# High and low weights of a merged product in alternating sets of two to four tile pairs

## The chip, the cores and the metric

One core of a Trainium2 chip runs the whole program once. The metric is the device time of that execution in microseconds (us), the median over several executions.

## The reference, cut to what matters

Two transformer blocks, one after the other, on 256 tokens of 1024 channels, all in float32. The first block has two layers (windowed attention, then a bidirectional retention), each with a gated feed-forward; the second has two layers of feed-forward, a three-branch mixer and another feed-forward:

```python
def swiglu_2(h, w_gate, w_up, w_down):
    return (jax.nn.silu(h @ w_gate) * (h @ w_up)) @ w_down
...
for l in range(DEPTH):
    x = x + 0.5 * swiglu_2(rmsnorm(x, ffn1_norm[l]), ffn1_w_gate[l], ffn1_w_up[l], ffn1_w_down[l])
    h = rmsnorm(x, mix_norm[l])
    proj = h @ w_in[l]
    ...
    x = x + 0.5 * swiglu_2(rmsnorm(x, ffn2_norm[l]), ffn2_w_gate[l], ffn2_w_up[l], ffn2_w_down[l])
```

Nearly all work is products of a 256-token activation with a large weight matrix. The hidden width of a feed-forward is 2816, so one feed-forward reads 1024x5632 and 2816x1024 weights.

## The kernel before

**Weights in two parts.** A float32 weight w is used as a high part `w_hi` (rounded by ScalarE, ACT) and a low part `w_lo` = w - w_hi (subtracted by VectorE, DVE). An activation has the same two parts. A product is high weight times high activation, plus high weight times low activation, plus low weight times high activation. Weights come in units: 4 chunks of 128 rows by 256 columns, one DMA of 512 KB into one of 4 slots (`raw`), from which ACT makes the slot's `w_hi` (line 1689) and DVE its `w_lo` (line 2328).

**A merged unit.** In the products `rg`, `rwo`, `gu1`, `dn1` of the first block and `gua`, `dna`, `memk`, `xr`, `yr`, `gub`, `dnb` of each layer of the second, the two activation parts lie so that one matmul takes both: it holds one 128x128 tile of `w_hi` and streams 512 columns, 256 of the high and 256 of the low activation (line 1086). These are called highs here. A low is a matmul that holds a tile of `w_lo` and streams the 256 high columns into the second half of the same bank (line 1097). A unit has 4 chunks k and 2 column blocks cb, so 8 tile pairs: 8 highs, a wait until DVE has made the unit's low weights (`unit_ready`, line 1009, semaphore lo_done), then 8 lows, the last of which counts the unit as used. Every matmul has its own weight load on the engine's load side (PEld).

**Which units there are.** `gua`, `gub`, `gu1` (gate and up of a feed-forward) have 11 iterations of 4 units; the first is written out, the other 10 are a loop on the chip. `dn1`, `dna`, `dnb` (down) have 2 iterations of 12 units, as a loop; the sixth and the twelfth unit of an iteration have 2 chunks, so 4 highs and 4 lows. `rg`, `rwo`, `xr`, `yr`, `memk` have 4 to 16 units. In `gua` and `gub` the sums of squares of the layer before (3 matmuls of line 1231) stand between units 2 and 3 of the first iteration. The first two units of `rg`, `gu1`, `gua`, `gub`, `xr` take chunk by chunk as the norm delivers them (`opens`), and the last unit of `rwo` goes by columns: 4 highs, 4 lows, 4 highs, 4 lows (lines 1042 and 1045).

**Order around it.** Each engine runs its own program in order. ACT and DVE split weights up to four units ahead of PE and take finished blocks of results in between; slots come free when PE has used a unit.

Of the kernel before, what the change touches and what calls it, by code (L numbers as in the profile page):

```python
# [26 lines left out]
P = 128  # L27
D = 1024
DC = D // P
S = 256  # L30
# [3 lines left out]
KCH = 4  # L34
# [336 lines left out]
def pooled_before(name, l):  # L371

    if name in SQUARED1:
        return 3 * (SQUARED1.index(name) - len(BOTH))
    return 3 * (len(SQUARED1) - len(BOTH) + SQUARED2.index(name) + l * len(SQUARED2))
# [7 lines left out]
def squared_before(name, l):  # L383

    first = [5 if n in BOTH else 4 for n in SQUARED1]
    if name in SQUARED1:
        return sum(first[:SQUARED1.index(name)])
    return sum(first) + 4 * SQUARED2.index(name) + l * 4 * len(SQUARED2)


def build(nc, a, out, const_at):
    J = JOBS
    st = ExitStack()
    with st:
        def sb(name, shape, dt=F32, on=st):
            return on.enter_context(nc.sbuf_tensor(name, shape, dt))

        def sem(name):
            return st.enter_context(nc.semaphore(name))
# [6 lines left out]
        w_hi = sb("w_hi", [P, SLOTS, KCH, COLS], F32R)  # L406
        w_lo = sb("w_lo", [P, SLOTS, KCH, COLS], F32R)
# [123 lines left out]
        units_used = sem("units_used")  # L531
# [143 lines left out]
        def norm_sums(n, half):  # L675

            return wk[:, 2 if half else 3, 0:S]
# [328 lines left out]
        def _(pe):  # L1006
            def unit_ready(job, l, it, p):

                pe.wait_ge(lo_done, job.split(l, it, p) + SLOTS + 1)
# [11 lines left out]
            def keep_busy(bank, n):  # L1021

                for _ in range(n):
                    pe.matmul(bank[:, 0:P], ident[:, :], ident[:, :], start=True, stop=True, skip_group_check=True)

            def product(name, l=None, hi=None, lo=None, tok=slice(0, S), rows_of=None, needs=None, normed=None, squared=False,
                        after=None, scaled=None, sums=None, merged=None, free=None,
                        sums_after=None, written=False, by_columns=False, busy=0):

                job = J[name]  # L1030
                per = job.body // job.per
                hi, lo = (h_hi, h_lo) if hi is None else (hi, lo)

                def one(it, start=0):
                    for p in range(start, job.body):
                        b, u = divmod(p, per)
                        if by_columns and (it, p) == (job.iters - 1, job.body - 1):
                            unit_ready(job, l, it, p)
                            for cb in range(2):
                                c = slice(cb * P, (cb + 1) * P)  # L1040
                                for k in range(job.unit_chunks[p]):
                                    pe.matmul(acc[:, b % 2, cb, :], w_hi[:, p % SLOTS, k, c], merged[:, :, u * KCH + k, tok], start=False, stop=False,
                                              skip_group_check=True)
                                for k in range(job.unit_chunks[p]):
                                    mm = pe.matmul(acc[:, b % 2, cb, S:2 * S], w_lo[:, p % SLOTS, k, c], merged[:, 0, u * KCH + k, tok], start=False,
                                                   stop=(k == job.unit_chunks[p] - 1), skip_group_check=True)
# [10 lines left out]
                        nk, s, last = job.unit_chunks[p], p % SLOTS, u == per - 1  # L1057
# [3 lines left out]
                        if tokens_major:  # L1061
                            unit_ready(job, l, it, p)
                            for n, r in enumerate(tokens_major):
                                packed = len(tokens_major) > 2
                                o = acc[:, b % 2, n // 2, (n % 2) * S:(n % 2) * S + S] if packed else acc[:, b % 2, n, 0:S]
                                for k in range(nk):
                                    x = slice(r * P, (r + 1) * P)
                                    kk = u * KCH + k
                                    for i, (xs, ws) in enumerate(((hi, w_hi), (hi, w_lo), (lo, w_hi))):

                                        mm = pe.matmul(o, xs[:, kk, x], ws[:, s, k, :],
                                                       start=(u == 0 and k == 0 and i == 0 and not (packed and n % 2)),
                                                       stop=(last and k == nk - 1 and i == 2), skip_group_check=packed)
                        else:
                            t = tok if not callable(tok) else tok(b)
                            outs = [acc[:, b % 2, cb, 0:t.stop - t.start] if merged is None else acc[:, b % 2, cb, :] for cb in range(2)]
                            opens = b == 0 and ((normed is not None and not isinstance(normed, tuple)) or (scaled is not None and isinstance(it, int)))
                            order = [(k, cb) for k in range(nk) for cb in range(2)] if opens else [(k, cb) for cb in range(2) for k in range(nk)]
                            for k, cb in order:
                                kk, c = u * KCH + k, slice(cb * P, (cb + 1) * P)  # L1080
                                if normed is not None and not isinstance(normed, tuple) and cb == 0 and b == 0:
                                    pe.wait_ge(h_ok, normed + kk + 1)
                                if scaled is not None and isinstance(it, int) and cb == 0 and b == 0 and kk % 2 == 0:
                                    pe.wait_ge(y_ok_c, scaled + kk // 2 + 1)
                                if merged is not None:
                                    pe.matmul(outs[cb], w_hi[:, s, k, c], merged[:, :, kk, t], start=(u == 0 and k == 0), stop=False,  # L1086
                                              skip_group_check=True)
                                else:
                                    for x in (hi, lo):
                                        pe.matmul(outs[cb], w_hi[:, s, k, c], x[:, kk, t], start=(u == 0 and k == 0 and x is hi), stop=False,  # L1090
                                                  skip_group_check=True)
                            unit_ready(job, l, it, p)
                            for cb in range(2):
                                o = outs[cb] if merged is None else outs[cb][:, S:2 * S]
                                x = hi if merged is None else merged[:, 0]
                                for k in range(nk):
                                    mm = pe.matmul(o, w_lo[:, s, k, cb * P:(cb + 1) * P], x[:, u * KCH + k, t], start=False,  # L1097
                                                   stop=(last and k == nk - 1), skip_group_check=True)
# [5 lines left out]
                if isinstance(normed, tuple):  # L1104

                    slot_free(job, l, 0, 0)
                    for half in range(2):
                        t = slice(half * S, half * S + S)
                        for p in range(per):
                            if not half:  # L1110
                                unit_ready(job, l, 0, p)
                            for cb in range(2):
                                for k in range(KCH):
# [5 lines left out]
                                    for i, (ws, xs) in enumerate(((w_hi, hi), (w_hi, lo), (w_lo, hi))):  # L1119
                                        mm = pe.matmul(acc[:, 0, cb, t], ws[:, p % SLOTS, k, c], xs[:, p * KCH + k, t],  # L1120
                                                       start=(p == 0 and k == 0 and i == 0),
                                                       stop=(p == per - 1 and k == KCH - 1 and i == 2), skip_group_check=True)
                            if half:
                                mm.then_inc(units_used, 1)
                    one(0, per)
                    for it in range(1, job.iters):
                        one(it)
# [95 lines left out]
            def pooled_sum(name, l=None):  # L1223

                pe.wait_ge(pooled, pooled_before(name, l) + 3)
                if name != "rwo":
                    pe.wait_ge(sqb_ok, squared_before(name, l) + 4)
                for n, src in enumerate((sq_of[:, 0, 0, :], sq_of[:, 1, 0, :], sq_of[:, 1, 1, :])):
                    if name == "rwo" and n:
                        pe.wait_ge(*((col_ok, 4) if n == 1 else (sqb_ok, squared_before(name, l) + 4)))  # L1230
                    mm = pe.matmul(norm_sums(None, 0), ones[:, :], src, start=(n == 0), stop=(n == 2))
                mm.then_inc(ss_ok, 1)
# [230 lines left out]
            def beside_queries(u):  # L1463
# [13 lines left out]
                if u == 6:  # L1477
                    query_sums(2)
                    partners(6)

            product("q0", tok=both, after=beside_queries, written=True)
            for k in range(3):
                side_modulation(k)
# [79 lines left out]
            for h in range(RH):  # L1563
# [3 lines left out]
                if h:  # L1567
# [3 lines left out]
                    after=lambda u: turn_y(RH - 1) if u == 0 else None)  # L1571
# [7 lines left out]
            for l in range(LAYERS2):  # L1579
# [10 lines left out]
                job = J["kvlru"]  # L1590
                slot_free(job, l, 0, 0)
                slot_free(job, l, 0, 1)
                for p in range(2):
                    unit_ready(job, l, 0, p)
                    for cb in range(2):
                        for k in range(KCH):
                            for i, (ws, xs) in enumerate(((w_hi, h_hi), (w_hi, h_lo), (w_lo, h_hi))):
                                mm = pe.matmul(acc[:, 1 - cb, 0, 0:S], ws[:, p, k, cb * P:(cb + 1) * P], xs[:, p * KCH + k, 0:S],
                                               start=(p == 0 and k == 0 and i == 0), stop=(p == 1 and k == KCH - 1 and i == 2))
                    mm.then_inc(units_used, 1)  # L1600
                for p in range(2, 4):
                    unit_ready(job, l, 0, p)
                    wh, wl = w_diag[:, p - 2, 0], w_diag[:, p - 2, 1]
                    for c in range(DC):
                        b = 2 * (p - 1) + c // 4
# [5 lines left out]
                        for i, (w, x) in enumerate(((wh, h_hi), (wh, h_lo), (wl, h_hi))):  # L1611
                            mm = pe.matmul(o, w[:, c * P:(c + 1) * P], x[:, c, mem], start=(i == 0), stop=(i == 2))
# [3 lines left out]
                for r in range(2):  # L1616
                    mm = pe.transpose(wk[:, 3, r * P:(r + 1) * P], v_T[:, r * P:(r + 1) * P], ident[:, :])
# [51 lines left out]
            job, l = J["dnb"], LAYERS2 - 1  # L1669
# [1557 lines left out]
```

## Time and profile before

| | |
|---|---|
| median of 3 runs | 2412.74 us (2411.22 to 2414.16) |
| profiled execution | 2409.69 us, of which the traced span is 2407.9 us |
| PE busy | 2370.9 us, 98% of the span, 14322 matmuls |
| DVE, ACT busy | 1557.6 us (65%), 1209.4 us (50%) |
| granted TensorE clock | 1.000 of full speed (2.4 GHz) as the mean over the span |

A profile's busy time of PE counts overlapping matmuls once. A matmul's own duration (start to end) is longer than its distance to the next one, because matmuls are pipelined.

### The profile page before, as it was taken

The numbers are of one execution on the slowest core, as the hardware profiler recorded it, in microseconds if no ns is written. First come the engines' busy times: TensorE is split into PE (matmuls) and PEld (weight loads), VectorE is DVE, ScalarE is ACT, GpSimd is POOL, SyncE is SP. The second block draws the span as 40 slices with busy tenths as digits, with TensorE's granted clock in tenths as the row PEclk, the third lists the DMA queues.
The fourth block names the chain that finished last, engine by engine and source line by source line (L and its number), as shares of the span: only waits on it lengthen the run. The fifth ranks groups of instructions, "written<-read, shape, count | busy, mean of one in ns | idle before, by whom it ended". The sixth has DMA issues, their size and how long they took to land.

```text
span 2407.9 us, 39768 instructions
## 1 busy us (share of the span) xinstructions
PE 2370.9 (98%) x14322; PEld 2029.7 (84%) x14322; DVE 1557.6 (65%) x2316; ACT 1209.4 (50%) x1783; POOL 158.1 (7%) x145
## 2 busy tenths in 40 slices
PE   8999999999999999999999999999999999999999
PEld 6756888888898868888888899998888889989887
DVE  5386665423474267766876858777677776777875
ACT  4365422222353234655554586565455556865553
POOL 3000100000000000000000013100000000221000
PEclk9999999999999999999999999999999999999999
DMA  9453755433363214656656655366566565545654
GB/s 332 135 184 128 228 154 162 143 107 96 99 193 96 88 53 154 204 163 195 201 173 193 192 168 176 130 181 193 178 191 193 180 196 167 183 130 158 200 174 149
DMA packets 388420, 398.39 MB, mean 165 GB/s; under 512 B 17344, under 2 KB 382432, under 8 KB 388304
## 3 DMA queue, kind: packets, MB, share of 16 engines
q1 hardware_dynamic: 381984, 377.67, 50.8%
q0 software_dynamic: 6320, 19.17, 2.6%
q8 instruction: 74, 1.21, 0.2%
q14 instruction: 42, 0.34, 0.1%
HBM read 395.73 MB, written 1.05 MB: 165 GB/s over the span
## 4 chain that ended last, share of the span: by engine, by line
PE 84%; DVE 5%; ACT 4%; issue 3%; POOL 2%; SPq 1%; DMA 1%; DVEq 0%; ACTq 0%; POOLq 0%
PE acc L1086 30%; PE acc L1097 23%; PE acc L1090 16%; PE acc L1163 2%; PE wk L1163 2%; ACT w_hi L1689 1%; DVE w_lo L2328 1%; SPq L795 1%; PE wk L1285 1%; PE acc L1639 1%; PE wk L1323 1%; PE acc L1323 1%; PE wk L1305 1%; POOL bias L994 1%; PE wk L1534 1%
## 5 line engine op out<-in xcount | busy, mean ns | idle before, releaser
L2328 DVE TENSOR_TENSOR w_lo<-raw,w_hi 128x1024 fp32r<-128x1024 f32 (+1 forms) x656 | 815.9, 1258 | 496.9 <-ACT w_hi L1689 495.1
L1689 ACT CAST w_hi<-raw 128x1024 fp32r<-128x1024 f32 (+1 forms) x650 | 663.8, 1034 | 466.8 <-PE acc L1097 346.1
L1086 PE MATMUL acc<-h_room,w_hi 128*128 128x512 f32 x2328 | 584.6, 393 | 2.0 <-DVE h_room L2579 0.8
L1097 PE MATMUL acc<-h_room,w_lo 128*128 128x256 f32 (+1 forms) x3688 | 562.0, 294 | 0.0
L1097 PEld LDWEIGHTS acc<-h_room,w_lo 128*128 128x128 f32 x3688 | 515.5, 188 | 44.7
L1086 PEld LDWEIGHTS acc<-h_room,w_hi 128*128 128x128 f32 x2328 | 415.5, 188 | 79.0 <-DVE h_room L2456 3.3
L1090 PE MATMUL acc<-h_room,w_hi 128*128 128x256 f32 (+1 forms) x2720 | 464.6, 323 | 3.2 <-POOL h_room L999 2.2
L1090 PEld LDWEIGHTS acc<-h_room,w_hi 128*128 128x128 f32 x2720 | 399.9, 188 | 47.7 <-issue 6.6
L1086 PE MATMUL acc<-hid_all,w_hi 128*128 128x512 f32 x880 | 221.4, 392 | 0.0
L1086 PEld LDWEIGHTS acc<-hid_all,w_hi 128*128 128x128 f32 x880 | 156.7, 188 | 26.7
L1097 PEld LDWEIGHTS acc<-hid_all,w_lo 128*128 128x128 f32 x1056 | 152.3, 188 | 16.7
L1097 PE MATMUL acc<-hid_all,w_lo 128*128 128x256 f32 (+1 forms) x1056 | 165.4, 297 | 0.0
L2625 DVE TENSOR_TENSOR act_buf<-acc,act_buf 128x512 f32<-128x512 f32 x110 | 75.9, 690 | 75.2 <-ACT act_buf L1973 52.0
L1090 PE MATMUL acc<-hid_all,w_hi 128*128 128x512 f32 x352 | 83.9, 390 | 0.0
L1090 PEld LDWEIGHTS acc<-hid_all,w_hi 128*128 128x128 f32 x352 | 65.9, 188 | 13.7
L1973 ACT COPY act_buf<-acc 128x512 f32<-128x512 f32 x55 | 32.2, 586 | 88.9 <-PE acc L1097 88.9
L1879 ACT ACTIVATE probs<-probs,soft_nm 128x257 f32<-128x257 f32 (+3 forms) x112 | 61.5, 554 | 20.2 <-DVE soft_nm L2497 17.1
L961 POOL TENSOR_TENSOR act_buf<-act_buf 128x512 f32<-128x512 f32 x8 | 10.4, 1296 | 847.9 <-ACT act_buf L1937 847.9
L2628 DVE TENSOR_TENSOR act_buf<-act_buf,rstd 128x512 f32<-128x512 f32 x88 | 60.9, 692 | 3.0
L1983 ACT CAST hid_all<-act_buf 128x512 f32 (+1 forms) x55 | 34.3, 623 | 54.6 <-DVE act_buf L2633 53.7
L1163 PE MATMUL wk<-w_hi,h_room 128*128 128x512 f32 x192 | 61.6, 397 | 0.0
L1971 ACT COPY act_buf<-acc 128x512 f32<-128x512 f32 x55 | 32.2, 585 | 51.8 <-PE acc L1097 51.6
(439 smaller groups left out, 2300.6 us busy)
## 6 DMA issues: line engine op xcount, KB each, us to landing
raw<-in_w_in_dram SPq DMA_DIRECT2D x100, 512.0 KB, 4.0
raw<-in_ffn_w_in_dram SPq DMA_DIRECT2D x88, 512.0 KB, 4.4
raw<-in_ffn_w_gate_dram SPq DMA_DIRECT2D x88, 512.0 KB, 4.2
raw<-in_ffn_w_up_dram SPq DMA_DIRECT2D x88, 512.0 KB, 4.3
raw<-in_ffn_w_down_dram SPq DMA_DIRECT2D x80, 512.0 KB, 4.0
raw<-in_ret_w_qkvg_dram SPq DMA_DIRECT2D x48, 512.0 KB, 3.6
raw<-in_ffn_w_out_dram SPq DMA_DIRECT2D x40, 512.0 KB, 3.5
ring<-in_ada_w_dram SPq DMA_DIRECT2D x34, 512.0 KB, 4.7
```

The lines of the kernel that those rows point to most:

```text
L1086: pe.matmul(outs[cb], w_hi[:, s, k, c], merged[:, :, kk, t], start=(u == 0 and k == 0), stop=False, skip_group_check=True)
L1090: pe.matmul(outs[cb], w_hi[:, s, k, c], x[:, kk, t], start=(u == 0 and k == 0 and x is hi), stop=False, skip_group_check=True)
L1097: mm = pe.matmul(o, w_lo[:, s, k, cb * P:(cb + 1) * P], x[:, u * KCH + k, t], start=False, stop=(last and k == nk - 1), skip_group_check=True)
L1163: mm = pe.matmul(banks[n], xs[:, kk, x], ws[:, 2 * u:2 * u + 2, k, :], start=(kk == 0 and i == 0), stop=(kk == DC - 1 and i == 2))
L1323: mm = pe.matmul(G["out"][:, seen], G["v"][c], G["probs_t"][:, 2 * (q % 2) + n, c, seen], start=(c == 0), stop=(c == tiles - 1), skip_grou ...
L1689: act.copy(w_hi[:, s, 0:nk, :], raw[:, s, 0:nk, :]).then_inc(hi_done, 1)
L1879: act.activation(pr, pr, ACT.Exp, bias=snm[:, i % 8:i % 8 + 1], accum_out=ssum[:, i % 8:i % 8 + 1])\
L1971: act.copy(buf, acc[:, 0, :, S:2 * S]).then_inc(low_ok, 1)
L1983: act.copy(hid_hi[:, bass.ts(it, 2), hid_tokens], buf).then_inc(hid_hi_ok, 1)
L2328: dve.tensor_tensor(w_lo[:, s, 0:nk, :], raw[:, s, 0:nk, :], w_hi[:, s, 0:nk, :], ALU.subtract).then_inc(lo_done, 1)
L2625: dve.tensor_tensor(part, acc[:, b, :, 0:S], part, ALU.add).then_inc(acc_free, 1)
L2628: dve.tensor_tensor(part, part, scale, ALU.mult).then_inc(gu_ok if b else gz_ok, 1)
```

## The change

A merged unit that is not opened chunk by chunk no longer does its 8 highs and then its 8 lows. Its 8 tile pairs are cut into three sets; of each set first the highs are issued, then the lows of the same pairs. The sizes are 3, 3, 2 and 2, 3, 3 in turn, 4, 2, 2 for the first such unit of a product or of a loop's body, and 2, 2 for a unit of two chunks. The wait for the low weights stands behind the first set's highs. The last unit of `rwo` stays as it was. In the loops of `rg`, `gu1` and `xr` the units that were opened chunk by chunk in every iteration are now so opened in the first alone. Numbers of matmuls, loads, waits on the weights and all other engines' programs are unchanged.

```diff
+            def set_sizes(job, first, p, anew):
+
+                good, sizes = True, []
+                for q in range(first, p + 1):
+                    if job.unit_chunks[q] < KCH:
+                        sizes = [2, 2]
+                    elif q == first and anew:
+                        sizes, good = [4, 2, 2], False
+                    else:
+                        sizes, good = [3, 3, 2] if good else [2, 3, 3], not good
+                return sizes
...
-                            opens = b == 0 and ((normed is not None and not isinstance(normed, tuple)) or (scaled is not None and isinstance(it, int)))
+                            opened = isinstance(it, int) and ((normed is not None and not isinstance(normed, tuple)) or scaled is not None)
+                            opens = b == 0 and opened
+                            if merged is not None and not opens:
+                                pairs = [(k, cb) for cb in range(2) for k in range(nk)]
+                                sizes = set_sizes(job, per if opened else 0, p, isinstance(it, int) or not (sums or busy or free))
+                                for g, n in enumerate(sizes):
+                                    some = pairs[sum(sizes[:g]):sum(sizes[:g]) + n]
+                                    for k, cb in some:
+                                        pe.matmul(outs[cb], w_hi[:, s, k, cb * P:(cb + 1) * P], merged[:, :, u * KCH + k, t],
+                                                  start=(u == 0 and k == 0), stop=False, skip_group_check=True)
+                                    if not g:
+                                        unit_ready(job, l, it, p)
+                                    for k, cb in some:
+                                        mm = pe.matmul(outs[cb][:, S:2 * S], w_lo[:, s, k, cb * P:(cb + 1) * P], merged[:, 0, u * KCH + k, t],
+                                                       start=False, stop=(last and k == nk - 1), skip_group_check=True)
+                                mm.then_inc(units_used, 1)
+                                if after:
+                                    after(it * job.body + p)
+                                if sums and isinstance(it, int) and p == 1:
+                                    pooled_sum(*sums)
+                                continue
```

PE's program at the start of `gub`, from the sums of squares on (units 3 and 4 of the first iteration, then the loop's first unit); before:

```order
L1231 MATMUL wk<-act_buf,ones 128x256 x2
L1086 MATMUL acc<-h_room,w_hi 128x512 [waits hi_done,acc_free]
L1086 MATMUL acc<-h_room,w_hi 128x512 x7
L1097 MATMUL acc<-h_room,w_lo 128x256 [waits lo_done]
L1097 MATMUL acc<-h_room,w_lo 128x256 x7
L1086 MATMUL acc<-h_room,w_hi 128x512 [waits hi_done]
```

The same place of the changed program, through unit 4:

```order
L1263 MATMUL wk<-act_buf,ones 128x256 x2
L1097 MATMUL acc<-h_room,w_hi 128x512 [waits hi_done,acc_free]
L1097 MATMUL acc<-h_room,w_hi 128x512 x3
L1102 MATMUL acc<-h_room,w_lo 128x256 [waits lo_done]
L1102 MATMUL acc<-h_room,w_lo 128x256 x3
L1097 MATMUL acc<-h_room,w_hi 128x512 x2
L1102 MATMUL acc<-h_room,w_lo 128x256 x2
L1097 MATMUL acc<-h_room,w_hi 128x512 x2
L1102 MATMUL acc<-h_room,w_lo 128x256 x2
L1097 MATMUL acc<-h_room,w_hi 128x512 [waits hi_done]
L1097 MATMUL acc<-h_room,w_hi 128x512
L1102 MATMUL acc<-h_room,w_lo 128x256 [waits lo_done]
```

Unit 3, the first after the sums, has become 4, 2, 2, and unit 4 begins with two highs, after which it waits for its low weights.

PE's program in the loop of `dn1`, one of its units of sizes 2, 3, 3 and the beginning of the next; before:

```order
L1086 MATMUL acc<-hid_all,w_hi 128x512 [waits hi_done]
L1086 MATMUL acc<-hid_all,w_hi 128x512 x7
L1009 REGISTER_ALU
L1097 MATMUL acc<-hid_all,w_lo 128x256 [waits lo_done]
L1097 MATMUL acc<-hid_all,w_lo 128x256 x7
```

and in the changed program:

```order
L1097 MATMUL acc<-hid_all,w_hi 128x512 [waits hi_done]
L1097 MATMUL acc<-hid_all,w_hi 128x512
L1009 REGISTER_ALU
L1102 MATMUL acc<-hid_all,w_lo 128x256 [waits lo_done]
L1102 MATMUL acc<-hid_all,w_lo 128x256
L1097 MATMUL acc<-hid_all,w_hi 128x512 x3
L1102 MATMUL acc<-hid_all,w_lo 128x256 x3
L1097 MATMUL acc<-hid_all,w_hi 128x512 x3
L1102 MATMUL acc<-hid_all,w_lo 128x256 x3
```

The wait for lo_done has moved from behind the eighth high to behind the second.

## Rows read from the trace of the kernel before

**Rows 1.** The page: share of each engine, PE's clock, and the chain by engine.

```profile
PE 2370.9 (98%) x14322; PEld 2029.7 (84%) x14322; DVE 1557.6 (65%) x2316; ACT 1209.4 (50%) x1783; POOL 158.1 (7%) x145
...
PEclk9999999999999999999999999999999999999999
...
PE 84%; DVE 5%; ACT 4%; issue 3%; POOL 2%; SPq 1%; DMA 1%; DVEq 0%; ACTq 0%; POOLq 0%
```

**Rows 2.** Busy us of PE, PEld, DVE, ACT, POOL in gub's loop; clock, DMA.

```profile
1594.00:1704.00 110.00, 110.00 (x640) 96.84 (x640) 89.75 (x103) 62.23 (x80) 0.00 (x0) 1.00 0.67 197
```

**Rows 3.** Timeline of PE, gub's loop: start, us, engine, line, operation, count.

```profile
1602.30 1.99 PE L1086 MATMUL acc<-h_room,w_hi 128*128 128x512 f32 x8
1604.13 1.11 PE L1097 MATMUL acc<-h_room,w_lo 128*128 128x256 f32 x8
1605.07 2.00 PE L1086 MATMUL acc<-h_room,w_hi 128*128 128x512 f32 x8
1606.91 1.07 PE L1097 MATMUL acc<-h_room,w_lo 128*128 128x256 f32 x8
1607.81 1.99 PE L1086 MATMUL acc<-h_room,w_hi 128*128 128x512 f32 x8
```

**Rows 4.** Single highs and runs of lows of those units: duration in ns, min/median/max.

```profile
L1086 PE MATMUL acc<-h_room,w_hi x1: 388/388/388, 1602.3 to 1602.3; 128*128 128x512 f32 x1
L1086 PE MATMUL acc<-h_room,w_hi x1: 392/392/392, 1602.5 to 1602.5; 128*128 128x512 f32 x1
L1086 PE MATMUL acc<-h_room,w_hi x1: 394/394/394, 1602.8 to 1602.8; 128*128 128x512 f32 x1
...
L1086 PE MATMUL acc<-h_room,w_hi x1: 392/392/392, 1603.9 to 1603.9; 128*128 128x512 f32 x1
L1097 PE MATMUL acc<-h_room,w_lo x8: 279/280/283, 1604.1 to 1605.0; 128*128 128x256 f32 x8
...
L1086 PE MATMUL acc<-h_room,w_hi x1: 394/394/394, 1606.7 to 1606.7; 128*128 128x512 f32 x1
L1097 PE MATMUL acc<-h_room,w_lo x8: 276/276/276, 1606.9 to 1607.7; 128*128 128x256 f32 x8
```

**Rows 5.** Timeline of PE, the last unit of rwo, by columns.

```profile
936.95 1.07 PE L1042 MATMUL acc<-h_room,w_hi 128*128 128x512 f32 x4
937.86 0.63 PE L1045 MATMUL acc<-h_room,w_lo 128*128 128x256 f32 x4
938.33 1.09 PE L1042 MATMUL acc<-h_room,w_hi 128*128 128x512 f32 x4
939.26 0.62 PE L1045 MATMUL acc<-h_room,w_lo 128*128 128x256 f32 x4
```

**Rows 6.** Of its second four highs the first, third, fourth; lows behind them: ns.

```profile
L1042 PE MATMUL acc<-h_room,w_hi x1: 397/397/397, 938.3 to 938.3; 128*128 128x512 f32 x1
...
L1042 PE MATMUL acc<-h_room,w_hi x1: 392/392/392, 938.8 to 938.8; 128*128 128x512 f32 x1
L1042 PE MATMUL acc<-h_room,w_hi x1: 394/394/394, 939.0 to 939.0; 128*128 128x512 f32 x1
L1045 PE MATMUL acc<-h_room,w_lo x3: 276/276/276, 939.4 to 939.6; 128*128 128x256 f32 x3
```

**Rows 7.** Unit 3 of gub, behind the sums: its fourth and fifth high.

```profile
L1086 PE MATMUL acc<-h_room,w_hi x1: 394/394/394, 1589.2 to 1589.2; 128*128 128x512 f32 x1
L1086 PE MATMUL acc<-h_room,w_hi x1: 388/388/388, 1589.4 to 1589.4; 128*128 128x512 f32 x1
```

**Rows 8.** Timeline of PE and DVE around units 4 and 10 of dn1's first iteration.

```profile
1078.48 1.22 DVE L2328 TENSOR_TENSOR w_lo<-raw,w_hi 128x1024 fp32r<-128x1024 f32 x1
1078.86 2.00 PE L1086 MATMUL acc<-hid_all,w_hi 128*128 128x512 f32 x8
...
1093.80 1.23 DVE L2328 TENSOR_TENSOR w_lo<-raw,w_hi 128x1024 fp32r<-128x1024 f32 x1 [0.97 <-ACT w_hi L1689]
1094.06 2.00 PE L1086 MATMUL acc<-hid_all,w_hi 128*128 128x512 f32 x8
```

## The prediction

> **What bounds the kernel now.** The page comes first: PE is busy for 98% of the span at full granted clock, and 84% of the chain that ended last is PE [rows 1]. In the loop of `gub` PE is busy for all of 110.00 us, DVE for 89.75, ACT for 62.23 [rows 2]. A loop like this is as long as its matmuls are far apart, so the change can only act through the distance of one matmul to the next, or through a wait.
>
> The timeline gives that distance. Eight highs take 1.83 us (1602.30 to 1604.13) and 1.84 (1605.07 to 1606.91). The eight lows behind them take 0.94 the first time and 0.90 the second [rows 3]; whole units take 2.77 and 2.74. So there are slow and quick lows, 0.04 us apart in eight by the groups, 0.03 by the units: I take 4.5 ns each, with 4 and 5 as bounds.
>
> Single durations show what decides it [rows 4]. Highs go round in three: 388, 392, 394, then 388 again. I call these places A, B, C. The first unit shown starts at A, so its eighth high is B (392), and its lows are slow (279 to 283). The next unit ends at C (394), and its lows are quick (276). Eight highs that end at C began at B: so eight slow lows behind B do not let the round go on to C; it resumes at B. Behind quick lows it resumes at A. That is why units alternate: from A a slow one, from B a quick one.
>
> The last unit of `rwo`, by columns, shows shorter groups. Four highs from A end at A again; the four lows behind take 0.47 us (937.86 to 938.33), slow. The next four highs begin with 397 and end with 392, 394, B and C [rows 6], and take 0.93 us against 0.91 for the first four [rows 5]. So slow lows behind A cost 0.02 us in the highs after it as well. The lows behind C are quick in this group of four too, 276 [rows 6].
>
> **The change part by part.** No matmul, load or transfer is added, and other engines' programs are the same. 395 units are cut into sets: 375 with eight pairs, 20 short ones in `dn1`, `dna`, `dnb` (two per iteration, ten iterations).
>
> *3, 3, 2 and 2, 3, 3.* From A the first reads A B C quick, A B C quick, A B slow; the second, if the round resumes at B, B C quick, A B C quick, A B C quick, and ends ready for A. Of 16 lows 14 are quick, before 8: 6 times 4.5 is 27 ns per two units, 13 per unit gained. That needs two things which the trace does not show: that two slow lows leave the round where eight do, and that a unit of 3, 3, 2 starts at A. The other way round, 2, 3, 3 from A reads A B slow, B C A slow, B C A slow, and 3, 3, 2 from B reads B C A slow, B C A slow, B C quick: 2 of 16 are quick, and 13 ns per unit are lost. Either order reproduces itself without end, so what a product's first set unit leaves behind decides for its whole loop.
>
> *4, 2, 2.* From A it reads A B C A slow, then the two 397s of rows 6, slow, then two more highs, slow; stepping the round on in this way I end at B, in step with the 2, 3, 3 that follows. But `gua` and `gub` come to it behind the sums of squares, and there the fourth high is C (394) and the fifth A (388) [rows 7]. So the lows behind the fourth are quick, then A B slow, B C quick, and the round is at A, where 2, 3, 3 is out of step. This holds for four products with 40 loop units each. I carry it on: 160 units by 13 ns, **+2.1 us**. The loop ends at B, the down products' 4, 2, 2 from B ends at A by the same steps, and they stay out of step: nine whole units +0.12 us, the 4, 2, 2 about +0.02, and each short unit -0.03 (two of its four lows become quick, 0.01, and the 397s behind it go, 0.02): +0.08 per iteration, ten iterations, **+0.8**. `rg` and `rwo`, 29 units out of step, **+0.4**; `memk`, `xr`, `yr`, 34 units, partly so, **+0.3**. In `gu1` waits of the first iteration set the round anew, which I can't step through: **0**, with 0.6 to either side (42 units by 13).
>
> *The earlier wait.* It stands behind 2, 3 or 4 highs in place of 8. The subtractions of DVE, in their order, belong to the units in order; two are later than the new place, both in `dn1`. Unit 4's ends at 1078.48 + 1.22 = 1079.70; PE starts the unit at 1078.86 and has its two highs issued 2/8 of 1.83 later, 1079.32: 0.38 us of waiting. Unit 10's ends at 1095.03; its start of 1094.06 and three highs give 1094.75: 0.28 [rows 8]. Together **+0.7 us**, which nothing hides, since PE's chain goes on through `dn1`. Behind each wait are the unit's other highs, and behind them DVE and ACT, which take the block. Everywhere else I find the low weights there by the unit's start; DVE has a fifth of the loop free [rows 2].
>
> *The units no longer opened chunk by chunk* (`rg`, `gu1`, `xr`, loop iterations): their waits were for norms long done, and the stream ran without a gap before; **0**. If PE were not the bound there, neither this nor the quick lows would count.
>
> The sum: 2.1 + 0.8 + 0.4 + 0.3 + 0 + 0.7 = **+4.3 us**. The profiled execution took 2409.69 us (span 2407.9, 1.8 around it), below the lowest of the three runs; the mean of all four is 2411.95. I add to that: 2416.
>
> A rule weighed. By the rows a high is 229 to 230 ns from the next (1.83/8, 1.84/8) and a low 113 to 118 [rows 3]. The Trainium skill's page "TensorE: Matmul & The Clock Gate", section "Back-to-back issue gap", gives a warm matmul's distance as its columns over 2.4 GHz plus 2.5 ns, whatever its neighbours, that is 216 and 109 ns as estimates, and so no change from a reordering. The trace does not agree: lows of one shape differ by their place.
>
> **The rivals.**
> *In step.* The 4, 2, 2 leaves B also behind the sums, or a quick group of four is not neutral. Then 349 whole units gain 13 ns, -4.5; the twenty short units give -0.6, and 26 units of 4, 2, 2, with three groups of slow lows and 397s, cost about 0.03 more than such units take now, +0.8; with the waits -3.6: 2408. For it: from A the steps end at B. Against it: rows 7.
> *No effect of order.* Distances depend on a matmul alone: +0.7, 2412.7. Against it, rows 3 and 4; it is the rule above.
> *Short groups are never quick.* If a group of two or three lows never is quick and each restarts the highs at 397, a unit has 8 slow lows in place of 4 on average (+18 ns) and three times the 20 ns of rows 5: 349 by 78 ns, +27, 2439. For it: nothing in the trace shows quick lows in a group of three. Against it: in rows 4 quick lows are quick from the first to the last, so length should not matter. It decides from about a third of the groups on.
>
> **How the numbers follow.** Out of step, as forecast: 0.42, 2413 to 2419. In step: 0.34, 2405 to 2411. No effect: 0.09. Never quick, wholly or in part: 0.15. A difference of 0.2% (4.8 us, about what a measurement here can tell from none) lies just outside both main cases. Faster gets 0.20 of the 0.34 of in step, since a little more than I count is enough there, and 0.03 for gains not seen; slower gets 0.14 of the forecast's 0.42 and 0.12 of never quick's 0.15; the rest, 0.51, is no difference. The range leaves out the long end of never quick and the best of in step: 2407 to 2421.
>
> **What would show it.** In the loops of `gua` and `gub`: two units in 5.54 us instead of 5.51, with durations of lows mostly 279 and above; in step, 5.49 and mostly 276. In `dn1`, PE waits for DVE's `w_lo` in two places, about 0.4 and 0.3 us. Behind the sums, quick lows behind the fourth high. Highs of 397 behind most runs would mean never quick. What would make the prediction wrong is the resumption of the round behind groups of two to four, which I have seen for four and eight alone.

## The result and the profile after

The changed kernel takes 2415.27 us (median; 2414.07 to 2417.83), the kernel before 2411.37 (2410.23 to 2414.16). The ratio is 1.0015, 95% interval [1.0009, 1.0021]: slower, by about 3.9 us. That is a small difference, but the interval leaves out 1. The forecast was +4.3 us. The profiled execution took 2414.69 us, of which the span is 2412.9.

The profile's page shows nothing of it: the busy shares are those of [rows 1].

```profile
PE 2375.0 (98%) x14322; PEld 2033.8 (84%) x14322; DVE 1559.1 (65%) x2316; ACT 1209.7 (50%) x1783; POOL 158.0 (7%) x145
```

The same stretch of `gub`'s loop as in [rows 2], busy us of PE, PEld, DVE, ACT, POOL: PE is busy throughout again, but only 637 matmuls fall into it in place of 640.

```profile
1594.00:1704.00 110.00, 110.00 (x637) 96.88 (x637) 89.98 (x104) 63.08 (x82) 0.00 (x0) 1.00 0.66 192
```

The timeline of PE in that loop (start, us, engine, line, operation, count), a unit of 3, 3, 2 and one of 2, 3, 3:

```profile
1640.35 0.85 PE L1097 MATMUL acc<-h_room,w_hi 128*128 128x512 f32 x3
1641.03 0.52 PE L1102 MATMUL acc<-h_room,w_lo 128*128 128x256 f32 x3
1641.39 0.85 PE L1097 MATMUL acc<-h_room,w_hi 128*128 128x512 f32 x3
...
1642.43 0.62 PE L1097 MATMUL acc<-h_room,w_hi 128*128 128x512 f32 x2
1642.89 0.39 PE L1102 MATMUL acc<-h_room,w_lo 128*128 128x256 f32 x2
1643.12 0.62 PE L1097 MATMUL acc<-h_room,w_hi 128*128 128x512 f32 x2
1643.57 0.40 PE L1102 MATMUL acc<-h_room,w_lo 128*128 128x256 f32 x2
...
1645.89 0.85 PE L1097 MATMUL acc<-h_room,w_hi 128*128 128x512 f32 x3
```

The two units take 5.54 us (1640.35 to 1645.89), where two took 5.51 before [rows 3]. Three lows take 0.36 us (1641.03 to 1641.39), 118 ns each by the starts of single matmuls. Single durations in ns (min/median/max) say which lows are quick. First a group of three, then the two at 1642.89:

```profile
L1102 PE MATMUL acc<-h_room,w_lo x3: 279/279/280, 1644.5 to 1644.7; 128*128 128x256 f32 x3
```

```profile
L1102 PE MATMUL acc<-h_room,w_lo x2: 276/276/276, 1642.9 to 1643.0; 128*128 128x256 f32 x2
```

So 2 lows of 16 are quick, where 8 were before: the loop is out of step, as the prediction calls it. Where that was decided is seen behind the sums of squares at the start of `gub`, PE's timeline and the duration of the four lows of the 4, 2, 2:

```profile
1590.30 1.28 PE L1097 MATMUL acc<-h_room,w_hi 128*128 128x512 f32 x4
1591.42 0.62 PE L1102 MATMUL acc<-h_room,w_lo 128*128 128x256 f32 x4
1591.88 0.62 PE L1097 MATMUL acc<-h_room,w_hi 128*128 128x512 f32 x2
1592.33 0.40 PE L1102 MATMUL acc<-h_room,w_lo 128*128 128x256 f32 x2
1592.57 0.62 PE L1097 MATMUL acc<-h_room,w_hi 128*128 128x512 f32 x2
1593.03 0.39 PE L1102 MATMUL acc<-h_room,w_lo 128*128 128x256 f32 x2
```

```profile
L1102 PE MATMUL acc<-h_room,w_lo x4: 276/276/276, 1591.4 to 1591.8; 128*128 128x256 f32 x4
```

The lows behind the fourth high are quick (276), the next two take 0.24 us (1592.33 to 1592.57), the last two 0.23 (1593.03 to the next unit's 1593.26): quick, slow, quick, and the round stands at A before a unit of 2, 3, 3.

In `dn1` the timeline of PE and DVE shows the first wait at its new place, and none at the second:

```profile
1078.01 4.09 DVE L2360 TENSOR_TENSOR w_lo<-raw,w_hi 128x1024 fp32r<-128x1024 f32 x4
...
1078.40 0.62 PE L1097 MATMUL acc<-hid_all,w_hi 128*128 128x512 f32 x2
...
1079.29 0.51 PE L1102 MATMUL acc<-hid_all,w_lo 128*128 128x256 f32 x2 [0.26 <-DVE w_lo L2360]
...
1092.98 1.82 DVE L2360 TENSOR_TENSOR w_lo<-raw,w_hi 128x1024 fp32r<-128x1024 f32 x2
...
1094.17 0.85 PE L1097 MATMUL acc<-hid_all,w_hi 128*128 128x512 f32 x3
...
1094.86 0.52 PE L1102 MATMUL acc<-hid_all,w_lo 128*128 128x256 f32 x3
```

Unit 4's two highs start at 1078.40, its lows at 1079.29: 0.89 us where two highs need 0.46 (1642.43 to 1642.89 above), so 0.43 are lost. Unit 10's lows come 0.69 us after its three highs, which is their own time (0.68 for the three from 1640.35 above); DVE was done at 1094.80 (1092.98 + 1.82), not at 1095.03 as before [rows 8].

Product by product, in us, from the end of the product ahead to the product's own end (worked out from the starts of single matmuls). Two profiles of each kernel stand here; the second ones come from the experiments below.

| product | before | after | forecast |
|---|---|---|---|
| `gua`, layer 0 | 123.54, 123.88 | 124.32, 124.03 | +0.5 |
| `gua`, layer 1 | 123.17, 123.16 | 123.71, 123.67 | +0.5 |
| `gub`, layer 0; 1 | 122.71, 122.71; 122.71, 122.64 | 123.14, 123.20; 123.16, 123.16 | +0.5 each |
| `dna`, `dnb` (four alike) | 60.77, 60.77 | 60.95, 60.95 | +0.16 each |
| `dn1` | 61.66, 61.66 | 62.32, 62.41 | +0.16, waits +0.7 |
| `gu1` | 129.98, 130.00 | 129.32, 129.33 | 0 |
| `rg` | 53.02, 53.05 | 53.23, 52.90 | +0.4 with `rwo` |
| `rwo`, with `rv` and the retention ahead of it | 179.04, 179.04 | 178.89, 178.91 | |
| `yr` (both alike) | 22.05, 22.05 | 22.19, 22.19 | +0.3 with `memk`, `xr` |
| `rq`, not changed | 22.61, 21.76 | 22.61, 21.76 | none |
| `w_out`, layer 0, not changed | 23.21, 23.23 | 23.95, 23.95 | none |
| `w_out`, layer 1, not changed | 23.21, 23.96 | 23.95, 23.95 | none |

All merged products together, with what stands ahead of them, take 1295.69 and 1296.04 us before, 1299.01 and 1298.59 after: +2.9 us between the means.

The trace after also shows that fewer units were cut than the change describes and the prediction counts: 3048 lows run on the changed line 1102, where 395 units would have 3080. The loop of `xr` has a single iteration, which the code treats like the written-out first one: its first two units are 8 highs and 8 lows as before, not opened in the first iteration alone, and its third is 4, 2, 2. So 4 of the 8 units of each `xr` are cut and not 6, and 391 units in all.

### The profile page after: what moved, and what is told of

The parts are those of the page before. It is cut to its first block, busy times and chain, and to the rows that moved or that the text cites. A ratio compares the mean times of both kernels' runs of the same rounds, so it can differ in the third digit from the quotient of the medians.

```text
span 2412.9 us, 39742 instructions
## 1 busy us (share of the span) xinstructions
PE 2375.0 (98%) x14322; PEld 2033.8 (84%) x14322; DVE 1559.1 (65%) x2316; ACT 1209.7 (50%) x1783; POOL 158.0 (7%) x145
## 4 chain that ended last, share of the span: by engine, by line
PE 83%; DVE 5%; ACT 4%; issue 3%; POOL 2%; SPq 1%; DMA 1%; DVEq 0%; ACTq 0%; POOLq 0%
PE acc L1097 28%; PE acc L1122 16%; PE acc L1102 14%; PE acc L1129 9%; PE acc L1195 2%; PE wk L1195 2%; ACT w_hi L1721 1%; DVE w_lo L2360 1%; SPq L795 1%; PE wk L1317 1%; PE acc L1118 1%; PE acc L1671 1%; PE wk L1355 1%; PE acc L1355 1%; PE wk L1337 1%
## 5 line engine op out<-in xcount | busy, mean ns | idle before, releaser
L1097 PE MATMUL acc<-h_room,w_hi 128*128 128x512 f32 x2168 | 629.6, 392 | 0.3 <-DVE h_room L3026 0.2
L1122 PEld LDWEIGHTS acc<-h_room,w_hi 128*128 128x128 f32 x2720 | 400.8, 188 | 47.7 <-issue 6.6
L1102 PEld LDWEIGHTS acc<-h_room,w_lo 128*128 128x128 f32 x2168 | 368.4, 188 | 67.1
L1102 PE MATMUL acc<-h_room,w_lo 128*128 128x256 f32 x2168 | 385.0, 279 | 0.0
L1097 PEld LDWEIGHTS acc<-h_room,w_hi 128*128 128x128 f32 x2168 | 349.1, 188 | 23.2 <-DVE h_room L3026 0.4
L1129 PE MATMUL acc<-h_room,w_lo 128*128 128x256 f32 (+1 forms) x1520 | 267.2, 317 | 0.0
L1097 PE MATMUL acc<-hid_all,w_hi 128*128 128x512 f32 x880 | 256.9, 392 | 0.0
L1129 PEld LDWEIGHTS acc<-h_room,w_lo 128*128 128x128 f32 x1520 | 225.8, 188 | 22.4
L1102 PE MATMUL acc<-hid_all,w_lo 128*128 128x256 f32 x880 | 158.5, 279 | 0.3 <-DVE w_lo L2360 0.3
L1097 PEld LDWEIGHTS acc<-hid_all,w_hi 128*128 128x128 f32 x880 | 141.1, 188 | 8.5
L1122 PE MATMUL acc<-hid_all,w_hi 128*128 128x512 f32 x352 | 83.9, 390 | 0.0
L1122 PEld LDWEIGHTS acc<-hid_all,w_hi 128*128 128x128 f32 x352 | 65.9, 188 | 13.6
L2005 ACT COPY act_buf<-acc 128x512 f32<-128x512 f32 x55 | 32.2, 586 | 88.4 <-PE acc L1102 88.4
```

What stands on the lines that cost most here:

```text
L1097: pe.matmul(outs[cb], w_hi[:, s, k, cb * P:(cb + 1) * P], merged[:, :, u * KCH + k, t], start=(u == 0 and k == 0), stop=False, skip_group_ ...
L1102: mm = pe.matmul(outs[cb][:, S:2 * S], w_lo[:, s, k, cb * P:(cb + 1) * P], merged[:, 0, u * KCH + k, t], start=False, stop=(last and k == ...
```

## The experiments

**E1: the other order of the sets, in four products.** Only the sizes behind 4, 2, 2 in `gua` and `gub` change, against the changed kernel.

```diff
-                good, sizes = True, []
+                early = job is J["gua"] or job is J["gub"]
+                good, sizes = anew or not early, []
...
-                        sizes, good = [4, 2, 2], False
+                        sizes, good = [4, 2, 2], early
```

> The changed kernel, but in the four gate/up products gua and gub the sizes behind 4, 2, 2 go on with 3, 3, 2 and not with 2, 3, 3; same number of sets, matmuls and waits. Theory (the place in the round decides): these products come into step; 40 loop units each go from 10 to 12 ns above those of before to 14 ns below, so each product takes 1.06 us less than in the changed kernel (about 0.6 less than before, gua of the first layer 0.3 less because of its later norm), all else stays; 4.2 us less than the changed kernel in all, about 2411.1. Rival (smaller groups cost by themselves): each product stays 0.43 to 0.55 us above before, 2415.3.

2411.21 us (2409.24 to 2412.65); against the kernel before 0.9994 [0.9985, 1.0003]. `gua` and `gub` take 122.98, 122.60, 122.10, 122.10, against the changed kernel's first profile -1.33, -1.11, -1.04, -1.06; all but the first meet the 1.06 to 0.05 (in the first, the wait for the norm was 0.3 us shorter as well). PE's timeline of two units in `gub`'s loop, begun at A:

```profile
1640.99 0.85 PE L1098 MATMUL acc<-h_room,w_hi 128*128 128x512 f32 x3
1641.68 0.50 PE L1103 MATMUL acc<-h_room,w_lo 128*128 128x256 f32 x3
1642.02 0.85 PE L1098 MATMUL acc<-h_room,w_hi 128*128 128x512 f32 x3
...
1643.74 0.62 PE L1098 MATMUL acc<-h_room,w_hi 128*128 128x512 f32 x2
...
1646.48 0.39 PE L1098 MATMUL acc<-h_room,w_hi 128*128 128x512 f32 x1
```

They take 5.49 us (1640.99 to 1646.48), and three lows 0.34 (1641.68 to 1642.02). The same matmuls in the same number of sets, in another order, are 14 ns per unit quicker than whole units and 26 quicker than the change. So the rival, that small groups cost by themselves, falls. Outside these products the instructions are those of the changed kernel, and yet some products differ: `gu1` takes 130.43 here, 1.11 more, and `dn1` behind it 61.90, 0.42 less, with the same wait for `w_lo`.

**E2: `dn1` whole again.** The rest is the changed kernel.

```diff
                                 sizes = set_sizes(job, per if opened else 0, p, ...)
+                                if name == "dn1":
+                                    sizes = [2 * nk]
```

> The changed kernel, but dn1 alone takes its units whole again: 8 highs, the wait, 8 lows. Theory (the earlier wait costs in dn1): the wait of 0.43 us behind the second high of unit 4 is gone, and dn1 goes from 62.32 us back to about 61.7; the first norm of gua, which came 0.3 us late, comes on time. Rival (dn1 loses by its places in the round, as dna and dnb do by 0.17 us each): dn1 loses only 0.17, 62.15, and the wait is found elsewhere.

2415.88 us, one execution. `dn1` takes 61.66, as before, and the timeline of PE shows the fourth unit without a wait:

```profile
1078.42 1.99 PE L1099 MATMUL acc<-hid_all,w_hi 128*128 128x512 f32 x8
1080.25 1.11 PE L1104 MATMUL acc<-hid_all,w_lo 128*128 128x256 f32 x8
```

So the change costs `dn1` 0.66 us in these profiles: 0.43 is the earlier wait, read above, and `dna` and `dnb` tell that about 0.18 is the places. One time of `dn1` proves little, since other waits come and go: in E3 and E4, where it has the instructions of the kernel before, it takes 62.67 and 62.11, because PE once waits 0.8 and 0.2 us for `w_hi`. What carries the reading is the wait for `w_lo`: it stands in all three profiles with the sets in `dn1` (two of the changed kernel, and E1) and in none of the five with whole units. The first norm of `gua` came 0.3 us sooner, as expected, but it proves nothing: the kernel before has it 0.33 later in its second profile, the changed kernel 0.29 sooner. The whole time says nothing here, since in this one execution `gu0` took 1.2 us more and `gu1` 1.1.

**E3: 512-column matmuls ahead of products that have none.** In the kernel before, ahead of the first matmul of `gates` and `attn_out`: two in the first layer, three in the second. The result is overwritten by the product's own first matmul.

```diff
+                            for _ in range({("gates", 0): 2, ("gates", 1): 3, ("attn_out", 0): 2, ("attn_out", 1): 3}.get((name, l), 0) ...):
+                                pe.matmul(acc[:, b % 2, 0, :], w_hi[:, s, 0, 0:P], h_all[...],
+                                          start=True, stop=True, skip_group_check=True)
                             for k, cb in order:
```

> The kernel before, with matmuls of 512 columns put ahead of two products that have only matmuls of 256: two ahead of gates and of attn_out in the first layer, three ahead of each in the second. Their results are overwritten by the product's first matmul. Theory (a stream of 256-column matmuls keeps the distance it begins with, 113.3 or 117.9 ns, and only 512-column ones move it to another place): in at least one of the layers gates falls from 67.84 us to 65.28 plus the highs added (0.46 or 0.69), so by 1.9 to 2.1, and attn_out with mem_out, 192 matmuls, by up to 0.87 less the highs; where the number is the wrong one, the product grows by the highs alone. Rival (the distance belongs to the product's tiles and operands): gates grows by 0.46 and 0.69.

The timeline of PE at `gates`, first layer with two highs, second with three:

```profile
1410.87 0.63 PE L1080 MATMUL acc<-h_room,w_hi 128*128 128x512 f32 x2
1411.34 2.05 PE L1093 MATMUL acc<-h_room,w_hi 128*128 128x256 f32 x16
...
1414.17 0.52 PE L1093 MATMUL acc<-h_room,w_hi 128*128 128x256 f32 x3
...
2044.87 0.86 PE L1080 MATMUL acc<-h_room,w_hi 128*128 128x512 f32 x3
2045.57 1.98 PE L1093 MATMUL acc<-h_room,w_hi 128*128 128x256 f32 x16
...
2048.29 1.98 PE L1093 MATMUL acc<-h_room,w_hi 128*128 128x256 f32 x16
```

and at `attn_out`:

```profile
1538.67 0.62 PE L1080 MATMUL acc<-h_room,w_hi 128*128 128x512 f32 x2
1539.13 1.98 PE L1093 MATMUL acc<-h_room,w_hi 128*128 128x256 f32 x16
...
2170.70 0.85 PE L1080 MATMUL acc<-h_room,w_hi 128*128 128x512 f32 x3
2171.39 2.04 PE L1093 MATMUL acc<-h_room,w_hi 128*128 128x256 f32 x16
```

A unit of 24 matmuls of 256 columns takes 2.72 us (2045.57 to 2048.29) or 2.83 (1411.34 to 1414.17), and all units of `gates` behind the first keep to theirs. At `gates` three highs bring the quick distance and two don't; at `attn_out` two do and three don't. So `gates` takes 68.31 us in the first layer and 65.99 in the second, highs included, where it took 67.84, and the rival falls: the distance is no property of the product. The gain of `attn_out` and `mem_out` in the first layer, 0.39, came to nothing: `w_out` behind them then waits longer for POOL (line 999), with 1.79 us from one matmul to the next in the trace instead of 1.36. The one execution took 2412.32 us; with one layer missed and the highs added this says little.

**E4: units cut in two at the quick place.** In `gua` and `gub` every second unit is 6, 2 instead of 8; all other units are whole. The edit is against the changed kernel.

```diff
+                if not (job is J["gua"] or job is J["gub"]):
+                    return [2 * job.unit_chunks[p]]
+                return ([6, 2] if p == 3 else [8]) if anew else [8] if p % 2 == 0 else [6, 2]
```

> Units whole as in the kernel before (8 highs, 8 lows), but in gua and gub every second unit is 6 highs, 6 lows, 2 highs, 2 lows: the last unit of the first iteration, and the second and fourth of the loop's body. Theory (place in the round): the 6 and the 8 lows are all quick, 2 of 16 slow; each of the four products takes 0.56 us less than before, 2.2 in all, about 2409.2. Rival (smaller groups cost by themselves): a unit that is cut in two takes more than one that isn't; 0.1 to 0.3 us more per product, about 2412.

2409.05 us (2408.36 to 2412.55); 0.9989 [0.998, 0.9998]. The four products take 0.55, 0.54, 0.57 and 0.61 less than in the first profile of before, 2.27 together. The timeline of PE in `gub`'s loop:

```profile
1641.57 1.53 PE L1091 MATMUL acc<-h_room,w_hi 128*128 128x512 f32 x6
1642.95 0.84 PE L1096 MATMUL acc<-h_room,w_lo 128*128 128x256 f32 x6
1643.63 0.62 PE L1091 MATMUL acc<-h_room,w_hi 128*128 128x512 f32 x2
1644.08 0.40 PE L1096 MATMUL acc<-h_room,w_lo 128*128 128x256 f32 x2
1644.32 2.00 PE L1091 MATMUL acc<-h_room,w_hi 128*128 128x512 f32 x8
```

Six lows in 0.68 us (1642.95 to 1643.63), 113 ns each; the two behind B in 0.24. Groups of two, three, six and eight go by the same places.

**E5 and E6: both kernels once more,** with no edit.

> The kernel before once more, for a second profile. In the first one w_out (unchanged by the change) ran its matmuls 113 ns apart behind a stall of 1.36 us, and in four profiles of other versions 118 ns apart behind the same stall. Theory (a stall's end sets the place, by chance): w_out takes 23.2 or 23.95 us in each layer, and need not be the same as before; then its 1.5 us are no effect of the change. Rival (the change moves w_out to the other place every time): 23.21 us in both layers again.

> The changed kernel once more, for a second profile. Where no stall comes in between, the products repeat to 0.02 us: gub 123.15, dna and dnb 60.95. Open is what stands behind a stall: w_out 23.95 again or 23.21, gu1 129.3 (in step, as in the first profile) or 130.4 (out of step, as in two other versions), the wait of 0.43 us in dn1 there again or not.

They took 2409.95 and 2414.28 us. What the sets decide repeats to some hundredths (the table), and so does the wait of 0.43 us in `dn1`. `w_out`, which has no sets, does not: in the second profile of before it is quick in the first layer and slow in the second. PE's timeline behind the wait for POOL, both layers of that one execution:

```profile
1562.43 2.08 PE L1090 MATMUL acc<-h_room,w_hi 128*128 128x256 f32 x16 [1.10 <-POOL h_room L999]
...
1565.25 1.98 PE L1090 MATMUL acc<-h_room,w_hi 128*128 128x256 f32 x16
...
2195.72 2.15 PE L1090 MATMUL acc<-h_room,w_hi 128*128 128x256 f32 x16 [1.08 <-POOL h_room L999]
...
2198.65 2.04 PE L1090 MATMUL acc<-h_room,w_hi 128*128 128x256 f32 x16
```

Ahead of the wait both layers run at the slow distance; behind it one is quick and one slow. The end of a stall thus sets the place anew, and not always to the same. `rq`, behind the waits of `rg`, takes 22.61 or 21.76 in both kernels. `gu1` takes 129.32 and 129.33 in the changed kernel, 130.43 in E1 and E2 with the same instructions up to there: in step, as in both profiles of the changed kernel, is one of its two outcomes. For `w_out` the other six profiles help: in E1 to E4, E7 and E8 it runs at the slow distance behind the wait in both layers, although in E3 and E4 all its instructions are those of the kernel before. So the slow outcome doesn't need the change.

**E7 and E8: every low at the quick place.** Highs and lows of a unit need not come in equal numbers: once both banks are begun, all 8 lows can follow 6 or 7 highs. For that the pairs go chunk by chunk here, not column block by column block.

```diff
+            W, X, Y, Z = ((8, 8),), ((6, 8), (2, 0)), ((7, 8), (1, 0)), ((6, 6), (2, 2))
+            V = ((2, 2), (2, 1), (3, 5), (1, 0))
+            Q, R, T = ((4, 4),), ((2, 2), (2, 2)), ((3, 4), (1, 0))
+            DOWN = (W, X, Y, W, X, Q, X, Y, W, X, Y, R)
+            PARTS = {"gua": (W, Z, W, Z), "gub": (W, Z, W, Z), "gu1": (V, W, Z, W), "rg": (Z, W, Z, W), "dna": DOWN, "dnb": DOWN,
+                     "dn1": (V, W, X, Y, W, T, W, X, Y, W, X, Q), "memk": (W, X, Y, W), "xr": (X, Y, W, Z), "yr": (W, Z, W, Z)}
...
+                                for h, n in parts(name, it, p):
+                                    row += [(w_hi, *next(highs)) for _ in range(h)] + [(w_lo, *next(lows)) for _ in range(n)]
```

Each pair is (highs, lows). E7 has E3's three highs ahead of `gates` in both layers as well, E8 hasn't.

> The whole of the theory in one kernel. Lows stand where the round is at its quick place: a unit is 8 highs and 8 lows, or 6 highs, 8 lows, 2 highs, or 7 highs, 8 lows, 1 high, and every body closes its round with one or two groups of 2 slow lows; in gu1, dn1, rg and xr a first unit of 2 highs, 2 lows, 2 highs, 1 low, 3 highs, 5 lows, 1 high, which by the steps that I found ends at B from wherever it began; three 512-column matmuls ahead of gates in both layers. By the steps, against the first profile of before: gua and gub -0.56 us each, dna and dnb -0.52 each (the lows of a pair ahead of its highs cost nothing), gu1 -0.55, dn1 -0.43, rg -0.2, memk, xr, yr -0.1 each, rq -0.85 (rg now ends at C), gates -1.87 each with the highs added: -10.7; up to 1 us of it goes into waits that come sooner. 2401.5 (2400 to 2404). Rival (smaller groups or mixed order cost by themselves): the merged products gain nothing, and only gates and rq are quicker, 2407.

> The kernel of the run by place without the three matmuls ahead of gates. Theory (PE bounds gates and what follows): 3.7 us more than that run, about 2405.2. Rival (the engines behind gates bound that stretch and the gain of gates goes into a longer wait in the attention): no difference.

E7: 2401.62 us (2400.53 to 2402.67), 0.9957 [0.9944, 0.9971]. E8: 2404.90 (2403.93 to 2409.94), 0.9975 [0.9963, 0.9986]. Both beat both kernels. In E8 all merged products take 1290.06 us, 5.6 and 6.0 less than in the two profiles of before, where the steps gave 6.1: `dna` and `dnb` 60.25 (-0.52), `dn1` 61.23 (-0.43), `gu1` 129.34 (-0.64). `yr` missed: 22.16, +0.11 instead of -0.11. The trace shows why: the one loop iteration of `xr` ran like its written-out first one, two whole units and then V and W, not X, Y, W, Z. It ends with 8 quick lows, so `yr` begins at A and its first 8 lows are slow. The timeline of PE in E7's `dnb`, units of 6 and 2 highs and of 7 and 1 (the nine are the first one's last two and the second one's seven):

```profile
1745.07 1.54 PE L1107 MATMUL acc<-hid_all,w_hi 128*128 128x512 f32 x6
1746.44 1.07 PE L1110 MATMUL acc<-hid_all,w_lo 128*128 128x256 f32 x8
1747.35 2.22 PE L1107 MATMUL acc<-hid_all,w_hi 128*128 128x512 f32 x9
1749.41 1.07 PE L1110 MATMUL acc<-hid_all,w_lo 128*128 128x256 f32 x8
```

and at its `gates`, which now begin quick in the first layer too:

```profile
1405.69 0.86 PE L1120 MATMUL acc<-h_room,w_hi 128*128 128x512 f32 x3
1406.39 1.98 PE L1133 MATMUL acc<-h_room,w_hi 128*128 128x256 f32 x16
...
1409.11 1.98 PE L1133 MATMUL acc<-h_room,w_hi 128*128 128x256 f32 x16
```

Between E8 and E7 lie 3.3 us where `gates` promised 3.7: PE bounds that stretch, and little of the gain goes into later waits, other than behind `attn_out` in E3. The rivals of both runs fall.

## Why the prediction was right

The mechanism and the sign were right: the place in the round decides, and the start of `gua` and `gub` puts them out of step. The size, +4.3 forecast and +3.9 between the medians, is in part luck: the terms of the sum measured 2.9 together, and about 1 us came from a product that the sum leaves out. Point by point:

- *PE's distances bound the kernel.* Yes: E4 and E8 shorten the time by the distances alone, and E1 takes back what they cost.
- *Out of step in `gua` and `gub`, +2.1.* Between the means of two profiles +0.47, +0.53, +0.46 and +0.49, together 1.94. E1 shows that the order of the sets behind the 4, 2, 2 decides it, and that in step the change would have taken 2411.2 there, no different from before.
- *The down products, +0.8.* `dna` and `dnb` +0.18 each; with as much for `dn1`, an estimate, 0.9.
- *`memk`, `xr`, `yr`, +0.3.* `yr` +0.14 twice, the others within 0.05: 0.3. The term counted two units of `xr` in each layer that were not cut. Behind the waits of `xr` even `yr` isn't fixed: with the same sets it takes 22.19 in one layer and 22.04 in the other of E1 and of E2.
- *`rg` and `rwo`, +0.4.* Mis-sized: `rg` +0.03 between the means, `rwo` -0.14. With the same sets the stretch of `rwo` takes 179.24 and 179.20 in E1 and E2; that waits set its place anew, as in `gu1`, is likely but was not traced.
- *`gu1`, 0, give or take 0.6.* -0.67 in both profiles, in step: at the bound. E1 and E2 show the other outcome, +0.44.
- *The earlier wait, +0.7.* Half right: 0.43 at unit 4, forecast 0.38; none at unit 10, forecast 0.28. DVE's end there, 1094.80, was 0.23 us earlier than before: I had kept the times of before for DVE's work, and it moved too.
- *Not counted: `w_out`.* I had looked at merged products only. A product with nothing but 256-column matmuls also has a quick and a slow distance. `w_out` takes 23.95 in both layers in both profiles of the changed kernel; in those of the kernel before it was quick in three of four places, 23.21 to 23.23. It has the same instructions and follows the same wait, and E3 and E4 show it slow without the change, so this 1.1 us between the means can't be put down to the change.

So the merged products give +2.9 us, and what is left of the 3.9 is about what `w_out` did in these profiles; that it did so in the timed executions isn't shown.

The rule that the prediction weighed does not agree with these traces. By columns alone a matmul of 256 would take 109 ns, an estimate from the formula in the Trainium skill, "TensorE: Matmul & The Clock Gate", section "Back-to-back issue gap"; the traces have 113 ns at best (2.72 us by 24), 118 else, and the rule would have E1, E4 and E8 change nothing. The formula has no term for a matmul's neighbours, but the section gives it for an isolated matmul, which the prediction doesn't say. For a stream of weight loads and matmuls it has about 131 ns at 512 columns, and that does not agree with these traces either, where they lie 229 apart.

## What to carry to other kernels

Where PE is busy without a gap, compare the starts of single matmuls, not their groups: two distances for one shape mean that the order of the matmuls can be worth something, here 0.25% for reordering alone and 0.4% with six matmuls added. Step the pattern through from the last place that fixes it to the loop's end before choosing an order; an order that is best from one place can be worst from another and, in a loop, stays so. Trust it only up to the next stall, or begin the loop with a sequence that ends at one place from wherever it began.

## What the runs showed of the hardware

- By the starts of single matmuls, 512-column matmuls with a weight load each go round in three distances, 226, 229 and 232 ns (places A, B, C); 256-column ones take 113.3 ns behind C and 117.9 behind A or B, whatever their number. The granted clock was 1.00 in the stretches of `gub`, `gates` and `w_out`.
- Quick lows leave the round at A. What n slow lows leave it at depends on 1 + n behind A and on 2 + n behind B, taken modulo 3. With 1 the round resumes at B. With 0 three highs take 235, 232 and 232 ns, and then comes A. With 2 two highs take 233 and 236, and then comes B. These steps gave `gub`, `dna`, `dnb` and `gates` in the kernels above to 0.1 us.
- A stream of 256-column matmuls alone never left its distance here: the 24 units of `gates` take 67.84 us or, with three 512-column matmuls ahead, 65.28 and 0.70 for those.
- The end of a stall sets the place, and not the same one in each execution. With `rq` (0.85 us), `w_out` (0.74 per layer) and `gu1` (1.1) this can spread one program's executions by some 3 us, as an estimate; those of the kernel before spread over 3.9. Why the round exists, and how a stall's end picks the place, stays open.
